# Two weight loads of the last expert, split into ten transfers each by rows

## The reference, cut to what matters

```python
gates, idx = lax.top_k(affinity, cap)            # cap = 32 tokens for each of 16 experts
xe = jax.vmap(lambda hb, ib: hb[ib])(h, idx)
hid = jax.nn.silu(jnp.einsum('becd,edf->becf', xe, w_gate)) * jnp.einsum('becd,edf->becf', xe, w_up)
ye = jnp.einsum('becf,efd->becd', hid, w_down) * gates[..., None].astype(h.dtype)
```

## Time and profile before

| | |
|---|---|
| median of 3 runs | 1679.0 us (1678.32 to 1680.46) |
| the profiled execution, its own time | 1677.46 us |
| its span, first to last instruction | 1675.7 us |
| mean granted TensorE clock | 0.915 |
| TensorE busy with matmuls | 1444.6 us, 86% |
| DMA, mean over the span | 354 GB/s |
| DMA, 1500 to 1600 us | 428 GB/s |

### The profile page before, as it was taken

The page is one execution under the profiler, slowest core; times in us unless marked ns, Lnnn a source line. Parts: engine busy times, 40 slices in busy tenths (PEclk is TensorE's granted clock), DMA queues, the critical chain, the costliest instruction groups (busy, mean ns, idle before and its releaser), DMA issues.

```text
span 1675.7 us, 19822 instructions
## 1 busy us (share of the span) xinstructions
PE 1444.6 (86%) x8024; PEld 859.2 (51%) x8024; DVE 712.7 (43%) x1150; ACT 328.2 (20%) x576; POOL 125.1 (7%) x113
## 2 busy tenths in 40 slices
PE   8999999999999999989777787776786677886886
PEld 6678778878888778875221241221332122332232
DVE  4446777678677877662212122102211211421122
ACT  3333333233333345530000000000000000000001
POOL 0000000004232244001000000000000000000002
PEclk8999999999999999999988888779889988877799
DMA  9997658656747765699999999999999999999997
GB/s 397 420 421 247 235 201 297 230 203 251 260 145 269 257 247 193 207 428 429 425 430 426 428 427 427 428 428 427 419 427 427 429 427 429 427 427 428 427 429 289
DMA packets 56228, 593.56 MB, mean 354 GB/s; under 512 B 6348, under 2 KB 6476, under 8 KB 8400
## 3 DMA queue, kind: packets, MB, share of 16 engines
q1 hardware_dynamic: 54584, 585.66, 85.7%
q10 hardware_dynamic: 1560, 6.67, 1.2%
HBM read 589.16 MB, written 2.10 MB: 353 GB/s over the span
## 4 chain that ended last, share of the span: by engine, by line
PE 54%; DMA 38%; DVE 4%; issue 2%; ACT 1%; POOL 1%; SPq 0%; POOLq 0%; DVEq 0%; ACTq 0%
DMA ring<-in_w_up 18%; DMA ring<-in_w_down 17%; PE bank L640 8%; PE bank L642 8%; PE bank L641 8%; PE bank L993 6%; PE bank L927 4%; PE bank L636 3%; PE bank L637 2%; PE bank L638 2%; PE bank L906 2%; PE bank L592 2%; PE bank L894 2%; PE bank L962 1%; DMA ring<-in_w_down_last 1%
## 5 line engine op out<-in xcount | busy, mean ns | idle before, releaser
L993 PE MATMUL bank<-ring,xg 128*32 128x512 f32 x1504 | 224.3, 728 | 119.1 <-DMA ring<-in_w_up 89.6
L1427 DVE TENSOR_TENSOR whl<-ring,whl 128x512 fp32r<-128x512 f32 x276 | 209.0, 759 | 130.0 <-ACT whl L1093 128.7
L1093 ACT ACTIVATE whl<-ring 128x512 fp32r<-128x512 f32 x276 | 173.4, 629 | 265.8 <-PE bank L642 210.4
L640 PE MATMUL bank<-whl,uh 128*128 128x512 f32 x512 | 206.4, 403 | 1.6 <-DVE vv L1456 0.9
L642 PE MATMUL bank<-whl,ul 128*128 128x512 f32 x512 | 199.8, 390 | 0.0
L641 PE MATMUL bank<-whl,uh 128*128 128x512 f32 x512 | 199.5, 390 | 0.0
L993 PEld LDWEIGHTS bank<-ring,xg 128*32 128x32 f32 x1504 | 46.1, 123 | 271.6 <-DMA ring<-in_w_up 138.4
L1410 DVE SCALAR_TENSOR_TENSOR part<-ring,csT,part 128x1024 f32<-128x1024 f32 x104 | 140.7, 1352 | 0.3 <-DMA ring<-in_w_mod_b 0.2
L1293 ACT ACTIVATE gup<-bank 128x512 f32<-128x512 f32 x32 | 18.7, 597 | 601.5 <-PE bank L993 601.5
L906 PE MATMUL bank<-yy,gcur 128*128 128x512 f32 x252 | 128.5, 634 | 4.9 <-DVE yy L1714 3.5
L1768 DVE COPY gup<-bank 128x512 f32<-128x512 f32 x32 | 22.0, 689 | 243.2 <-PE bank L993 243.1
(11 more groups left out here) (263 smaller groups left out, 1624.2 us busy)
## 6 DMA issues: line engine op xcount, KB each, us to landing
ring<-in_w_up SPq DMA_DIRECT2D x61, 2048.0 KB, 26.6
ring<-in_w_gate SPq DMA_DIRECT2D x33, 2048.0 KB, 25.8
ring<-in_w_mod_b SPq DMA_DIRECT2D x63, 1024.0 KB, 5.8
ring<-in_w_down SPq DMA_DIRECT2D x30, 2048.0 KB, 26.0
ring<-in_w_in SPq DMA_DIRECT2D x53, 1024.0 KB, 4.9
ring_b<-in_w_gate SPq DMA_DIRECT2D x15, 2048.0 KB, 21.3
ring_c<-in_w_gate SPq DMA_DIRECT2D x15, 2048.0 KB, 23.7
ring<-in_w_mod_a SPq DMA_DIRECT2D x28, 1024.0 KB, 16.3
```

What stands on the lines that cost most here:

```text
L640: mm(ps, hi[:, k, cols], wh, start=k == 0, stop=False)
L993: last = mm(bank[2 * m + half][32 * kk:32 * kk + 32, :], xg[:, 4 * j + kk, CAP * ei:CAP * ei + CAP], parts[kk // of][0][:, kk % of, 512 * ...
L1093: a(whl[:, cidx % (AHEAD + 1), 0, :], slot_buf(slot[n])[:, 512 * (k % 4):512 * (k % 4) + 512], ACT.Copy).then_inc(hi_split, 1)
L1427: v.tensor_tensor(whl[:, cidx % (AHEAD + 1), 1, :], slot_buf(slot[n])[:, 512 * (k % 4):512 * (k % 4) + 512], whl[:, cidx % (AHEAD + 1), 0, ...
```

## The change

The last expert's items 6 and 7 (w_up, quarters 2 and 3) are each loaded by ten transfers. Six of them take 16 rows: rows r, r+8, r+16, ... for r = 0 to 5. Four take 8 rows: rows r, r+16, r+32, ... for r = 6, 14, 7, 15. Together these are the 128 rows, and source and destination rows are the same as before. Each transfer raises `ring_full` by 16, so TensorE waits for 144 more on the two buffers.

```diff
+SHARED_ROWS = [slice(r, P, 8) for r in range(6)] + [slice(r, P, 16) for r in (6, 14, 7, 15)]
...
-        return pair_buf(d), ring_full[2 * d], g * (16 * 8) + (fills[2 * d] + 16 * (2 * ei + n // RING + 1))
+        more = 16 * (len(SHARED_ROWS) - 1) if is_final(g, ei) and i in (6, 7) else 0
+        return pair_buf(d), ring_full[2 * d], g * (16 * 8) + (fills[2 * d] + 16 * (2 * ei + n // RING + 1) + more)
...
         for i in range(6, 8):
             sp.wait_ge(moe_used, 12 * (E - 1) + i - RING + 1)
-            expert_item(E - 1, i, i - 4)
+            d = moe_pairs[(i - 4) % RING]
+            for rows in SHARED_ROWS:
+                sp.dma_start(pair_buf(d)[rows, :], w_up[E - 1, i % 4][rows, :]).then_inc(ring_full[2 * d], 16)
```

## The result

The changed kernel takes 1698.84 us (median of 4 runs, 1697.9 to 1699.56), the kernel before 1679.16 us (4 runs, 1678.32 to 1680.46). The ratio is 1.0119, interval 1.0106 to 1.0131: 19.7 us slower. Forecast was 1687.0, with a range from 1677.3 to 1690.0. The sign and the mechanism held, the size did not.

The account below looks back on a forecast made before the run. The prediction took the weight stream's last landing as the bound. Split items at 13.9 GB/s an engine move it by +8.1 us: 1677.46 + 8.1 = 1685.6, plus 1.5 to the shown median, forecast 1687, range 1677.3 to 1690.

Parts of the forecast that it names:

- What bounds the kernel: Expert half: one stream of weights through 16 busy engines; the end hangs on the engine that drains last, at 1661.71.
- The rate of the split items: Loads of items 6 and 7: 13.9 GB/s an engine, from `b_row`'s 223 GB/s, instead of 26.75 at full rate.
- the doubt named beside it: `b_row`'s slow stretch might come from reading the same few DRAM rows repeatedly, and then would not carry over.
- the term of the sum: Items 6 and 7: early engine's 20 rows take 23.6 us, +13.8; late engine's 14.1, +4.3; last landing +8.1.
- the shift: Over items 6 and 7, eight engines carry 20 rows and eight 12, instead of 16: 2.45 us moved at full rate.
- SP: Twenty issues on SP's queue replace two: 10.2 us, at worst 17.2; cover 7.6 us, at worst 0.7, so no cost.
- `fw`: Its load stands behind the issues on SP: 4.8 us of issue against 8.8 us of cover, so no cost.
- Which half gets more: The 8-row transfers of items 6 and 7 use the early engines; using the late half would move its end 2.45 us.
- TensorE's wait for item 7: Before item 7 on TensorE: data there at 1649.8, 6.5 us after the former start at 1643.31.
- The balance rival: Split rows go at full rate, halves end at 1658.4 and 1659.3, waits of 1.28 us vanish: 1677.7; chance 0.34.

Follow-up runs that it names:

- e8: The kernel before, with `b_row` read from 128 different rows of DRAM instead of four repeated ones: 1678.74 us against 1679.6 unedited.
- e10: Changed kernel with only item 6 split, into eight transfers of 16 rows, 8 apart, item 7 in one: 1688.49 us against 1680.3 for the kernel before.
- e2: Changed kernel with eight transfers an item of 16 rows, 8 apart, so every engine carries equal rows: 1693.94 us, +16.2 over the kernel before.
- e1: Changed kernel with the same destination rows but consecutive source rows of DRAM: 1695.78 us against 1677.73 for the kernel before.
- e3: Changed kernel with sixteen transfers an item of 8 rows, 4 apart: 1697.41 us, +19.7 over the kernel before.
- e4: Changed kernel with sixteen transfers an item of 8 rows, 16 apart: 1709.0 us, +31.3 over the kernel before.
- e11: Changed kernel with an item as 64 rows (step 2), 32 rows (step 4) and four 8-row transfers (step 4): 1688.86 us against 1680.3 for the kernel before.
- e6: Changed kernel with two transfers an item, even rows and odd rows: 1678.05 us against 1679.6 for the kernel before.
- e9: Changed kernel with four transfers an item of 32 rows, every fourth row: 1678.46 us against 1680.3 for the kernel before.
- e12: Changed kernel with each item as even and odd rows, timed in five rounds: 1678.05 us against 1678.66 for the kernel before, ratio 0.9994.
- e5: Changed kernel with two transfers an item, rows 0 to 63 and 64 to 127: 1692.6 us against 1679.6 for the kernel before.
- e7: Changed kernel with eight transfers an item of 16 neighbouring rows: 1697.69 us against 1679.6 for the kernel before.

## Why the prediction was right in sign and wrong in size

**What bounds the kernel: right.** The stream of weights and its last landing set the end; the last landing and the span moved by the same 20.9 us.

**The rate of the split items: right.** 13.9 GB/s an engine (223 / 16) was taken, 223 / 16 was measured over 32 us. The row of `b_row` gave the right size, though that it is the very same figure is luck: its windows ran from 223 to 260. e8 removes the doubt named beside it. The 361 GB/s of `part<-mrow` didn't carry over; whether that is because the copy is short or because it reads the few partitions, no run shows. By the Trainium skill, "SBUF — State Buffer", Door 1: The DMA port swizzle, the estimate was 13.6 GB/s an engine; the trace agrees.

**The step that failed is the term of the sum: +13.8 us for an early engine and +4.3 for a late one.** It slowed only the rows of the split items, 9.05 us for an average engine. The profile shows 15.3 us. The prediction had written that beside `b_row` "every engine is slowed, not only its own", and then the sum left the neighbours out. In the change 7.1 million bytes went at the low rate and 4.19 were expected; item 5 is late by 3.56 us although it is an ordinary transfer; e10 shows 2.10 of 4.86. Two smaller terms are missing:

- The ends. From the windows above the mean engine ends at 1670 + 4 x (0.91 + 0.32 + 0.09) = 1675.3, and the last 7.3 us later. Before, with shares of 0.65 and 0.31 in the two windows shown below, the mean is 1654 + 4 x 0.96 = 1657.8, and the last 3.9 us later. The shift was to narrow the ends; they widened by 3.4 us. The completions in the trace show how: of the sixteen engines, two complete j = 7 at 1671.3, twelve from 1674.9 to 1676.5, one at 1680.2 and one at 1682.6. e2, without the shift, ends in two halves of eight, 1672.3 to 1673.6 and 1676.5 to 1678.2. So the shift did draw the halves together, and two engines that fell behind took more than it gave. In e1, e3, e4 and e11, the other kernels with pieces of 8 rows, two engines also end some 2 to 4 us behind their group. Why they fall behind is open.
- The start. Item 6 was issued at 1619.19, 1.1 us later than in the profile of before, which no step of the change explains; between the experiments' executions that start lies anywhere from 1617.55 (e3) to 1620.95 (e11).

```profile
1654.00:1658.00 4.00, 3.90 (x24) 0.99 (x20) 1.99 (x3) 1.41 (x4) 2.54 (x3) 1.00 0.65 272
1658.00:1662.00 4.00, 2.71 (x18) 0.61 (x18) 1.30 (x3) 0.76 (x3) 1.81 (x2) 1.00 0.31 127
```

With 0.7 us for 1658 to 1662, where 354 GB/s moved, the sum is 15.3 + 0.7 + 3.4 + 1.1 = 20.5 of the 20.9 us. The forecast's +8.1 fell short by 12.8: the neighbours are 6.3 of that (15.3 against 9.05), and the ends 4.4, since the forecast had them narrow by 1.0.

**SP: off by a third, harmless.** 13.2 us against 10.2: a 16-row issue costs 0.67 us (10.79 us for the 16 of e2) and not the 0.40 taken from 128-row rows. The cover held, since slow engines need j = 0 later. In e3, with 32 issues, it didn't: eight engines stood idle.

**`fw`: harmless, but not for the reason given.** The forecast set 4.8 us of issue against 8.8 us of cover. The rows came 20.4 us later, not 4.8; what needs them moved as well, by 21.5, and the cover in the end was 9.6 us (1674.84 less 1661.79 and 3.45).

**Which half gets more: right.** In e3 eight engines complete item 5 from 1628.65 to 1629.52, the other eight from 1631.45 on. The first completions of item 6's 8-row pieces come from 1629.26 on, 0.61 us after the first of these and before the other eight have ended item 5: the early half carries them.

**TensorE's wait for item 7: 6.5 us forecast, 3.52 measured**, because items 5 and 6 had already cost 3.56 and 6.47 us. What ran at half clock ran while TensorE had time to spare; the end hung on the landing.

**The balance rival** needed full rate while rows were written in this pattern. No run gave it that: each way to move rows to the early engines makes them write partitions of the others.

## What to carry to other kernels

Before a load is split, ask which partitions its engines write at one moment, and beside whom: transfers of 64 and 32 rows with steps of 2 and 4 kept full rate (e6, e9, e12), halves, blocks of 16 and steps of 8 and 16 halved it (e2, e4, e5, e7), and so did 8 rows with a step of 4 once they went to the other half (e3). Cost the slow stretch with everything that flies beside the split load, not with the load's own bytes; here that was 7.1 million instead of 4.2. And where a row of the profile says that neighbours suffer, they belong in the sum.

## What the runs showed of the hardware that was not expected

- The low rate is about half whatever the pattern: 223, 214, 219, 209 and 193 GB/s for the change, e2, e5, e4 and e7. Why four groups are not slower than eight is open. The engines drift apart, so that more groups are in use at a moment than one transfer has; that is argued, not shown.
- Eight engines that write another half's partitions run at full rate, 213 GB/s, as long as the other eight are idle, and two such engines beside fourteen with ordinary transfers hold all at 203 GB/s (e3).
- Pieces of one size and one step, on the same engines, take 0.61 us a row for partitions 0 to 63 and 1.22 to 1.3 us for partitions 64 to 127, while the other eight engines are at work (e3).
- Splitting by even and odd rows costs nothing: 0.9994, interval 0.9985 to 1.0002 (e12).
